# A scan's odd-head products turned to the other chunk's partitions, and its state read from a ring

## What is computed

```python
def step(state, inp):
    r_t, w_t, k_t, v_t, a_t, b_t = inp
    sa = jnp.einsum('bhvk,bhk->bhv', state, a_t)
    state = (state * w_t[:, :, None, :] + sa[..., None] * b_t[:, :, None, :]
             + v_t[..., None] * k_t[:, :, None, :])
    y_t = jnp.einsum('bhvk,bhk->bhv', state, r_t)
...
y = (y - mean) * lax.rsqrt(var + GN_EPS)
y = y.reshape(B, S, RWKV_DIM) * ln_w.astype(f32) + ln_b.astype(f32)
bonus = jnp.sum(r * k * r_k.astype(f32), axis=-1, keepdims=True) * v
y = (y + bonus.reshape(B, S, RWKV_DIM)) * g.astype(f32)
```

## Time and profile before

| | us |
|---|---|
| median of 3 runs (lowest, highest) | 1550.77 (1547.91, 1551.12) |
| the profiled execution | 1551.75 |
| its span, first to last instruction | 1549.2 |
| scan rounds | about 617 to 720 |
| last y tiles, g products, first branch products | about 720 to 758 |

### The profile page before, as it was taken

How to read it: one execution, slowest core, us unless ns; L and a number is a source line. 1 busy time by engine, 2 the same in 40 slices (tenths; PEclk the granted TensorE clock), 3 DMA queues, 4 the chain that set the end, 5 groups by cost and what they waited for, 6 DMA issues and landing times.

```text
span 1549.2 us, 26173 instructions
## 1 busy us (share of the span) xinstructions
PE 1505.4 (97%) x10293; PEld 1215.7 (78%) x10293; DVE 1079.8 (70%) x1776; ACT 659.2 (43%) x1165; POOL 98.5 (6%) x181
## 2 busy tenths in 40 slices
PE   6999999999999999999999999999999999999998
PEld 5976666787777887888787887888888888887876
DVE  6468986467787581577866469777777747877786
ACT  7544454344433212445423236444444533433453
POOL 1010000000010001255100020000000000000000
PEclk9999999999999999999999999999999999999999
DMA  5030000713222535302357213444444689878754
GB/s 195 14 78 28 1 1 3 203 41 106 65 69 65 161 129 131 103 4 68 114 162 261 75 55 129 151 151 153 155 155 146 215 307 326 298 279 279 272 188 150
DMA packets 176752, 212.41 MB, mean 137 GB/s; under 512 B 28645, under 2 KB 110946, under 8 KB 176002
## 3 DMA queue, kind: packets, MB, share of 16 engines
q1 hardware_dynamic: 176574, 210.91, 41.1%
q10 hardware_dynamic: 68, 0.02, 0.0%
HBM read 154.11 MB, written 54.82 MB: 135 GB/s over the span
## 4 chain that ended last, share of the span: by engine, by line
PE 67%; DVE 16%; DMA 10%; issue 3%; SPq 2%; ACT 2%; POOL 0%; DVEq 0%; ACTq 0%; POOLq 0%
PE bank L3255 19%; PE bank L2856 11%; DMA down_raw<-in_w_ff_down 7%; PE bank L3167 5%; PE bank L3220 5%; PE bank L3319 5%; PE bank L2756 3%; PE bank L2716 2%; PE bank L2649 2%; PE bank L2769 2%; PE bank L2784 2%; DVE xprod L2067 2%; DVE mg_lo L2483 2%; DVE mg_hi L2481 2%; PE bank L2794 1%
## 5 line engine op out<-in xcount | busy, mean ns | idle before, releaser
L2856 PE MATMUL bank<-uT_hi,w_hi 128*128 128x512 f32 x432 | 171.3, 396 | 0.0
L2856 PE MATMUL bank<-uT_hi,w_lo 128*128 128x512 f32 x432 | 168.2, 389 | 0.0
L2856 PE MATMUL bank<-uT_lo,w_hi 128*128 128x512 f32 x432 | 168.2, 389 | 0.0
L3319 PE MATMUL bank<-mg_lo,mg_hi 128*128 128x512 f32 x576 | 135.2, 390 | 2.1 <-DVE mg_lo L2483 1.9
L3319 PEld LDWEIGHTS bank<-mg_lo,mg_hi 128*128 128x128 f32 x576 | 107.7, 188 | 26.3 <-DVE mg_lo L2483 4.0
L3319 PE MATMUL bank<-yh,mg_lo 128*128 128x512 f32 x384 | 118.7, 390 | 0.5 <-DVE yl L2483 0.4
L1260 ACT ACTIVATE zbuf<-bank 128x512 f32<-128x512 f32 x54 | 32.4, 599 | 181.7 <-PE bank L2856 177.7
L2856 PEld LDWEIGHTS bank<-uT_hi,w_hi 128*128 128x128 f32 x432 | 81.1, 188 | 21.9 <-issue 5.2
L1607 ACT ACTIVATE f<-f 128x512 f32<-128x512 f32 x64 | 40.5, 632 | 131.6 <-DVE f L2435 69.6
L2856 PEld LDWEIGHTS bank<-uT_hi,w_lo 128*128 128x128 f32 x432 | 81.1, 188 | 17.3 <-issue 1.0
L2856 PEld LDWEIGHTS bank<-uT_lo,w_hi 128*128 128x128 f32 x432 | 81.1, 188 | 17.0
(11 more groups left out here) (498 smaller groups left out, 3772.7 us busy)
## 6 DMA issues: line engine op xcount, KB each, us to landing
down_raw<-in_w_ff_down SPq DMA_DIRECT2D x80, 512.0 KB, 5.4
down_raw<-f_spill SPq DMA_DIRECT2D x56, 512.0 KB, 4.0
f_spill<-x SPq DMA_DIRECT2D x80, 256.0 KB, 2.6
w_raw<-in_w_in SPq DMA_DIRECT2D x28, 512.0 KB, 4.1
sgate<-gate_spill SPq DMA_DIRECT2D x16, 512.0 KB, 4.3
up_a<-in_w_ff_up SPq DMA_DIRECT2D x16, 512.0 KB, 4.7
up_b<-in_w_ff_up SPq DMA_DIRECT2D x16, 512.0 KB, 4.2
f_spill<-f SPq DMA_DIRECT2D x32, 256.0 KB, 2.3
```

The costliest lines, as they stand in the source:

```text
L2856: ins = nc.tensor.matmul(ps[2 * slot + g][:], st[:, slot, k, :], mv[:, k, g * HALF:(g + 1) * HALF], start=(k == 0 and m == 0), stop=(k == ...
L3319: ins = nc.tensor.matmul(ps[4 * (q % 2) + t][:], st, mv_, start=(start and w == 0 and m == 0), stop=(stop and w == 1 and m == 2))
```

## The change

The odd head's chunk m is now written to the partitions of chunk 1 - m (`turned`), into a bank of its own: `mv` and `solve_mv` use bank 3 for the even and bank 4 for the odd head, `y_product` bank 7 and the upper half of bank 6, with bank 4 for the odd head of tile 6, and banks 6 and 5 for tile 7. The engines that empty these banks move the odd head back: `w_evac` is three copies (even head, then the odd head's two halves), `tw_evac` two, `u_add` reads the odd head's `taw` turned, `y_center` has two reductions and three subtractions. `solve_a` goes in two halves into the free columns of banks 1 and 2, with four copies where there were two. The state's output term is a step of its own, `y_state`: 16 products of 64x64 straight from `state`, which is now a ring of six; `statebd` and `spread_state` are gone. `naturals(j+1, 0)` moves from behind `u_product` to the end of the round before, `y_product` is no longer split, and the third and fourth g product wait for `y_center(6)` and `y_center(7)`. In ScalarE's order `nat_evac(j+1, 0)` stands between `tat_evac(j, 1)` and `tw_evac(j, 1)`. GpSimd's and SyncE's waits are renumbered. The core of the diff:

```diff
 
-        def y_bank(i):
-
-            return 6 if i == NT - 1 else 7
+        def y_part(i, h):
+
+            bank, o = ((6, 0), (5, 0))[h] if i == NT - 1 else ((7, 0), (4, 0))[h] if i == NT - 2 else ((7, 0), (6, 256))[h]
...
+        def turned(h, m):
+
+            return slice(CH * (m ^ h), CH * (m ^ h) + CH)
...
@@ -1005,19 +1014,6 @@
 
                 def bonus(i):
                     return bonus_last[:, i - (NT - 2), :] if i >= NT - 2 else bonus_odd[:] if i % 2 else rope_t[:].rearrange("p a h j -> p (a h j)")
-
-                def spread_state(k):
-
-                    pool.wait_ge(s_st, k + 1)
-                    if k >= 4:
-                        pool.wait_ge(s_ym, (k - 4) // 2 + 1)
-                    for h in range(2):
-                        r = slice(64 * h, 64 * h + 64)
-                        ins = nc.gpsimd.tensor_scalar(statebd[r, k % 4, :, r], state[r, k % 2, :, :], 1.0, 0.0, ALU.mult, ALU.add)
-                        if h == 0:
-                            pch(pool, ins)
...
                 def w_evac(i, hs):
                     n = 2 * i + hs
                     act.wait_ge(s_wm, n + 1)
-                    nc.scalar.activation(wv[:, n % 2, :], ps[3][:, 0:256], ACT.Copy).then_inc(s_we, 1)
+                    to = by_pair(wv[:, n % 2, :])
+                    src = [ps[3 + h][:, 0:P].rearrange("p (q v) -> p q v", v=RH) for h in range(2)]
+                    nc.scalar.activation(to[:, :, 0], src[0], ACT.Copy)
+                    for m in range(2):
+                        ins = nc.scalar.activation(to[turned(0, m), :, 1], src[1][turned(1, m)], ACT.Copy)
+                    ins.then_inc(s_we, 1)
 
                 def tw_evac(i, hs):
                     n = 2 * i + hs
                     act.wait_ge(s_twm, n + 1)
                     if i >= 2:
                         act.wait_ge(s_us, 2 * (i - 1))
-                    nc.scalar.activation(taw[:, i % 2, hs * 256:(hs + 1) * 256], ps[3][:, 256:512], ACT.Copy).then_inc(s_tw, 1)
-
-                def tat_evac(i):
-                    act.wait_ge(s_tam, i + 1)
-                    for m, src in enumerate((ps[4][:, 0:256], ps[6][:, 256:512])):
-                        nc.scalar.activation(tat[:, i % 2, m], src.rearrange("p (c t) -> p c t", t=CH), ACT.Copy).then_inc(s_tat, 1)
+                    for h in range(2):
+                        ins = nc.scalar.activation(by_pair(taw[:, i % 2, hs * 256:(hs + 1) * 256])[:, :, h],
+                                                   ps[3 + h][:, P:2 * P].rearrange("p (q v) -> p q v", v=RH), ACT.Copy)
+                    ins.then_inc(s_tw, 1)
+
+                def tat_evac(i, hs):
+                    act.wait_ge(s_tam, 2 * i + hs + 1)
+                    if i >= 2:
+                        act.wait_ge(s_us, 2 * (i - 1))
+                    for m in range(2):
+                        nc.scalar.activation(tat[:, i % 2, m, 2 * hs:2 * hs + 2], ps[1 + m][:, 384:512].rearrange("p (c t) -> p c t", t=CH),
+                                             ACT.Copy).then_inc(s_tat, 1)
 
                 def square_y(i):
...
                         tw_evac(j, 0)
                     if i >= 2:
                         root_y(i - 2)
                     if j < NT:
                         nat_evac(j, 3)
                         w_evac(j, 1)
-                        tat_evac(j)
+                        tat_evac(j, 1)
+                        if j + 1 < NT:
+                            nat_evac(j + 1, 0)
...
                                             ALU.mult).then_inc(s_st, 1)
 
                 def y_center(i):
                     dve.wait_ge(s_ym, i + 1)
-                    y3 = ps[y_bank(i)][:].rearrange("p (h v) -> p h v", v=RH)
-                    dch(dve, nc.vector.tensor_reduce(small[:, 32:40], y3, AXX, ALU.add))
+                    y = [y_part(i, h).rearrange("p (c v) -> p c v", v=RH) for h in range(2)]
+                    nc.vector.tensor_reduce(small[:, 32:36], y[0], AXX, ALU.add)
+                    dch(dve, nc.vector.tensor_reduce(small[:, 36:40], y[1], AXX, ALU.add))
                     dch(dve, nc.vector.tensor_scalar(small[:, 32:40], small[:, 32:40], 1.0 / RH, None, ALU.mult))
                     if i >= 3:
                         dve.wait_ge(s_ytm, i - 2)
-                    nc.vector.tensor_tensor(yc[:, i % 3, :].rearrange("p (h v) -> p h v", v=RH), y3,
-                                            small[:, 32:40].unsqueeze(2).to_broadcast([P, NH, RH]), ALU.subtract).then_inc(s_yc, 1)
+                    to = yc[:, i % 3, :].rearrange("p (c h v) -> p c h v", h=2, v=RH)
+                    nc.vector.tensor_tensor(to[:, :, 0], y[0], small[:, 32:36].unsqueeze(2).to_broadcast([P, RC, RH]), ALU.subtract)
+                    for m in range(2):
+                        at = turned(1, m)
+                        ins = nc.vector.tensor_tensor(to[turned(0, m), :, 1], y[1][at],
+                                                      small[at, 36:40].unsqueeze(2).to_broadcast([CH, RC, RH]), ALU.subtract)
+                    ins.then_inc(s_yc, 1)
 
                 def y_var(i):
...
@@ -2969,6 +2981,8 @@
 
                 def products(i, hs):
 
+                    if i and hs == 0:
...
@@ -2995,7 +3009,7 @@
                         for h in range(2):
                             for m in range(2):
                                 rows = slice(CH * m, CH * m + CH)
-                                ins = nc.tensor.matmul(ps[3][rows, (2 * q + h) * RH:(2 * q + h + 1) * RH],
+                                ins = nc.tensor.matmul(ps[3 + h][turned(h, m), q * RH:(q + 1) * RH],
                                                        mq[h][rows, i % 3, 2 * hs + q, 1, :],
                                                        nat[rows, i % 3, 2 * hs + q, 3, h * RH:(h + 1) * RH], start=True, stop=True)
                     ins.then_inc(s_wm, 1)
...
                         for h in range(2):
                             for m in range(2):
                                 rows, v0 = slice(CH * m, CH * m + CH), (2 * q + h) * RH
-                                ins = nc.tensor.matmul(ps[3][rows, 256 + v0:256 + v0 + RH], tt[rows, 16 * (2 * hs + q) + 2 * i + h, :],
+                                ins = nc.tensor.matmul(ps[3 + h][turned(h, m), P + q * RH:P + (q + 1) * RH], tt[rows, 16 * (2 * hs + q) + 2 * i + h, :],
                                                        wv[rows, (2 * i + hs) % 2, v0:v0 + RH], start=True, stop=True)
                     ins.then_inc(s_twm, 1)
 
-                def solve_a(i):
-
-                    pe.wait_ge(s_nat, RC * (i + 1))
-                    if i:
-                        pe.wait_ge(s_tat, 2 * i)
-                        pe.wait_ge(s_us, 2 * i)
-                    for c in range(RC):
+                def solve_a(i, hs):
+
+                    pe.wait_ge(s_nat, RC * i + 2 * hs + 2)
+                    for h in range(2):
+                        pe.wait_ge(s_m[h], 2 * i + 2)
+                    if i or hs:
+                        pe.wait_ge(s_tat, 2 * (2 * i + hs))
+                    for c in (2 * hs, 2 * hs + 1):
                         for m, h in tiles:
-                            rows = slice(CH * m, CH * m + CH)
-                            bank, o = ((4, 0), (6, 256))[m]
-                            ins = nc.tensor.matmul(ps[bank][64 * h:64 * h + 64, o + c * CH:o + (c + 1) * CH],
+                            rows, o = slice(CH * m, CH * m + CH), 384 + (c % 2) * CH
+                            ins = nc.tensor.matmul(ps[1 + m][64 * h:64 * h + 64, o:o + CH],
                                                    nat[rows, i % 3, c, 0, h * RH:(h + 1) * RH], tt[rows, 16 * c + 2 * i + h, :],
                                                    start=True, stop=True)
                     ins.then_inc(s_tam, 1)
...
                         pe.wait_ge(s_us, n)
+                    if m and i >= 2:
+                        pe.wait_ge(s_yc, i - 1)
...
-                def y_product(i, c0, c1):
-                    yb = ps[y_bank(i)]
-                    if c0 == 0:
-                        pe.wait_ge(s_us, 2 * i + 2)
-                        pe.wait_ge(s_sbd, 2 * i + 1)
-                        if 1 <= i < NT - 1:
-                            pe.wait_ge(s_yc, i)
-                        if 2 <= i < NT - 1:
-                            pe.wait_ge(s_yt, min(i - 1, NT - 4))
-                    for c in range(c0, c1):
+                def y_state(i):
+                    pe.wait_ge(s_us, 2 * i + 2 if i == NT - 1 else 2 * i + 3 if i == NT - 2 else 2 * i + 4)
+                    pe.wait_ge(s_st, 2 * i + 2)
+                    if 1 <= i < NT - 1:
+                        pe.wait_ge(s_yc, i)
+                    if 2 <= i < NT - 1:
+                        pe.wait_ge(s_yt, min(i - 1, NT - 4))
+                    for b in range(0, RC, 2):
                         for m in range(2):
-                            r = CH * m
```

(78 more changed lines are left out.)

## The result

The changed kernel takes 1557.49 us (median; 1555.01 to 1559.55) against 1549.93 for the kernel before (1547.91 to 1551.12): ratio 1.0053, 95% interval 1.0037 to 1.0069, some 8 us more. The prediction said 1549.4 and no change that can be measured, and the time lies above its range.

The account below looks back on a forecast made before the run. The prediction took TensorE and VectorE to decide each scan round in turn, then TensorE after the tail. Scan -6.6 and tail +5.2 gave -1.4 us, so a median of 1549.4, range 1545.5 to 1556.5.

Parts of the forecast that it names:

- The price of four quarters: Small products in `mv`, `solve_mv` and `y_product`: 0.035 us each on four quarters of the array, 0.024 less than on two.
- Rival 4: Small products of the scan: four quarters help less, 0.05 us each, net +5.8 us, 1556.6; chance 0.08.
- The tail's wait: Behind the scan: the fourth g product waits 4.23 us for `y_center(7)`; with longer `y_center`s and signal +4.8 us.
- rival 2: Second `products` of rounds 2 to 6: the clock falls, 1.7 us each; with four falls 1556.2; chance 0.2.
- the scan: The rounds ahead of the tail: TensorE's savings less VectorE's longer work, -6.6 us in sum.
- TensorE's part: From a round's second `products` to the end of the next `u_product`: -1.5 us per full round.
- VectorE's part: From the end of `u_product` to the second `products`, with late `taw` copy for `u_add`: +0.64 us a round.
- y_center ... +0.50: VectorE in each round: two reductions and three subtractions instead of one each, +0.50 us.
- The main case: The likeliest case for the whole kernel: 1549.4 us, reaching from 1547 to 1552, chance 0.4.
- From there to the end of the next round's `u_product` TensorE decides: From a round's second `products` on, TensorE alone sets the time, 10.34 us before the change.
- GpSimd at nobody's cost: GpSimd in the scan: loses its copies of the state, two of them 0.89 us a round, without effect on others.
- Rival 3: ScalarE becomes the limit: copy pieces at full length, +0.8 us in six rounds, net +3.4, 1554.2; chance 0.1.

Follow-up runs that it names:

- e1: The kernel before, with only the third and fourth g product also waiting for the sixth and seventh y_center: 1553.72 us against 1550.00, ratio 1.0021.
- e3: The changed kernel with twelve idle products ahead of the second `products` of rounds 2 to 6: ratio 1.0052 to the kernel before.
- e6: The changed kernel with the odd head's pieces of `wv`, `usb` and `yc` left on their partitions; single run, scan and tail 222.1 us against the changed kernel's 225.8.
- e8: The kernel before with only `mv` and `solve_mv` turned, `solve_a` in halves and their pieces: 1547.28 us against 1550.65, ratio 0.9982.
- e10: The e8 kernel with GpSimd's `make_bonus` moved behind the copy of the state: 1545.88 us against 1549.84 before, ratio 0.9981.
- e11: The kernel before with only GpSimd's `make_bonus` moved behind the copy of the state: ratio 0.9998.
- e2: The changed kernel with only the last two g products in banks 4 and 5, the others in 1 and 3: ratio 1.0036 to the kernel before.
- e4: The changed kernel with `y_state`'s products reordered so that no quarter is used twice in a row: ratio 1.0058 to the kernel before.
- e7: The changed kernel with e2's banks, e4's order, `naturals(j, 0)` back at the round's head and `y_product` split: ratio 1.0008 to the kernel before.
- e9: The e7 kernel with all the even head's y products before the odd head's, two quarters at a time: ratio 1.0010 to the kernel before.
- e12: The changed kernel with six idle products ahead of the second `products` of rounds 2 to 6; single run, 1561.64 us.
- e5: The changed kernel with thirty more wait instructions on TensorE ahead of the scan; single run, scan and tail 231.3 us against the changed kernel's 225.8.

## Why the prediction was wrong, step by step

**Right.** *The price of four quarters*: `mv` 0.25 (0.28 forecast), y products 0.99 (1.1), and without the idle time the TensorE part of a round is 9.02 against 8.84 forecast. Rival 4 is out. With it goes the rule that the prediction weighed, 25 ns from one matmul's start to the next (the Trainium skill, TensorE: Matmul & The Clock Gate, section "Wait — 56ns, not 53.3ns?"): the trace does not agree, the matmul records of the y products start 15.5 ns apart (64 in 0.99 us). *The tail's wait*: the fourth g product waits for `yc`, e1 gives the wait alone 3.6 us, and 1.3 came back at `yin_lo`, as forecast. From the second `products` of the last round on, forecast were +5.2 less 1.5, measured +3.4. That this sum is so close is partly luck, for its terms are off: the wait itself is 2.3 instead of 4.2, since the first g product already waits 2.4 for ScalarE instead of 0.5, and there are two falls of the clock more than before (three against one) where one more was counted, while e1 shows the wait alone with none more. *The place and the mechanism of rival 2*.

**Wrong: the scan.** Forecast were -1.7 up to the first second `products` that waits, and -3.4 in the four rounds; measured +0.6 and +5.2. For the four rounds the terms can be set side by side:

| term, four rounds | forecast | measured |
|---|---|---|
| TensorE's part at full clock, without idle time (e3) | -6.0 | -5.7 |
| VectorE's part | +2.6 | +4.4 |
| one operation held up by GpSimd | 0 | +0.8 |
| idle time without a releaser (2.5 against 0.3) | 0 | +2.2 |
| clock, what is left of after's second parts against e3's | 0 | +3.4 |
| sum | -3.4 | +5.1 (the rounds show +5.2) |

1. *"y_center ... +0.50"* is the term that was mis-sized: +0.8 to +0.91, with +0.10 for the `usb` pair and 0.14 for `taw`, up to 1.16 in all for 0.64. I took the start-to-start distance from the `usb` pair of before, in which both operations lie on the same 64 partitions. The two last subtractions lie on different halves and move data between them, and they overlap with nothing (e6).
2. *"no round of before shows a fall"* was the argument against rival 2, and I had put the wait at 4.05 us and the work in it at 2.4. With term 1 it is 4.57, and there the clock falls in three of five rounds. The main case and rival 2 were not alternatives. Where the first part of a round lasts 3.6 us or less (before, e1, e8, e10, e11) none of 25 rounds has a fall; where it lasts 4.2 or more, with no filler in it (after, e2, e4 to e7, e9), 14 of 35 have one; with filler (e3, e12) none of 10. That the idle wait brings the falls is shown by the filler; that a longer first part by itself makes one likelier fits the counts, and no run tests it alone. The price of a fall, 1.7, was high: 0.9 to 1.3 measured, against e3.
3. *"From there to the end of the next round's `u_product` TensorE decides"* left out a third decider. Stretches of dense small products run TensorE out of instructions. In the last five rounds of before nothing stands still for this reason, so no row of the rounds priced it; the sign was in the same trace ahead of them, 1.15 us in the inverse's products (615.66). The change packs 32 y products, 8 of `mv` and 8 of `solve_a` into 1.5 us, and the supply doesn't follow. e5 moved the place, and the packets' times fix its end. In two rounds the same pause, 0.34 and 0.22 us, falls into `y_state`. Not settled is why the delay from packet to work is 2.1 to 2.9 us.
4. *GpSimd at nobody's cost* held for the copies that were removed, but its other work collided once in the four rounds. VectorE and GpSimd of after:

```profile
695.34 1.14 DVE L2168 TENSOR_SCALAR small<-small 128x8 f32<-128x8 f32 x1
```

```profile
695.18 1.27 POOL L1027 TENSOR_TENSOR rope_t<-rope_t,lnb 128x512 f32<-128x512 f32 x1
```

This operation takes 0.17 to 0.30 in the other rounds. It ends at 696.48, GpSimd's at 696.45, and the wait behind it is the longest, 2.57.

Rival 3 did not decide: `wv` is at full length (0.85 for its three pieces, 0.64 forecast), but only one wait of 0.7 for it shows.

What the change gains is real where it doesn't lengthen the engine that waits in turn with TensorE. `mv` and `solve_mv` are evacuated by ScalarE, which has room, and e10 shows 0.82 a round less than before and 0.67 less than e11, which has the same order on GpSimd; forecast was 0.77. The outputs are evacuated by VectorE inside TensorE's wait, and cost there more than they bring.

Open are how much of e2's tail is the clock, and the part of e12's total behind the tail.

## What to carry to other kernels

Price the evacuation on the engine that takes turns with TensorE before the products: here 0.77 us a round saved on TensorE cost 0.8 to 0.9 on VectorE, and only the half evacuated by an engine with room was a gain. Leave work in a long wait of TensorE: a fall of the clock behind it costs about 1 us. Idle products in the wait kept the clock up and shortened the rounds, but neither kernel that had them was faster as a whole (e3 1559.54, e12 1561.64 in one run, after 1557.49). After packing small products densely, look for idle time with no releaser, and whether its place drifts from round to round and its end follows a packet of instructions: that is the supply of instructions, and its place moved here with the number of instructions (e5), not with the data.

## What the runs showed of the hardware

- The 64x64 f32 y products and those of `mv` go at 0.031 us each on four quarters (two matmul records of 15.5 ns), against 0.060 and 0.059 on two. In `y_state` it hardly matters whether pairs share two quarters: 30 records in 0.66 us, 29 in 0.62 with the other order (e4).
- Dense stretches of small products make TensorE idle for up to 2.5 us; the idle time ends 2.1 to 2.9 us after a 16 KB packet of instructions, in 33 of 38 cases, and thirty more instructions ahead move its place by 14 or 15 records.
- Neighbouring operations on VectorE and ScalarE overlap by about 0.1 us; they don't if they lie on different halves of the partitions or one moves data between halves (e6).
- While GpSimd runs a 128x512 operation on two tensors of SBUF (1.27 us), a state update takes 1.33 instead of 0.42, and a 128x8 operation 1.14 instead of 0.17 to 0.30. The Trainium skill (SBUF — State Buffer, section "SBUF: two separate sides") calls the port pair that the two engines share an exclusive lock, held for the whole instruction; the ends at 696.45 and 696.48 agree. Moving the other work of GpSimd in e10 took away the 0.5 us waits of e8.
